# Head sums of squares: the two halves of the tokens in different columns of the array

## The chip, the cores and the metric

The kernel runs on one core of one Trainium2 chip. The metric is the device time of one execution in microseconds (us): the median of 3 runs of the kernel before is 2346.19 us (2345.56 to 2347.66). TensorE is called PE in the profile, its weight loads PEld, VectorE is DVE, ScalarE is ACT, SyncE is SP, GpSimd is POOL.

## The reference

One layer of a hybrid block on 1024 tokens of width 1024: adaLN, RMSNorm and one wide input projection that feeds dilated-window attention and a recurrent branch (RG-LRU); both are projected, gated, merged and added to x; then an expert-choice layer of 16 SwiGLU experts. All of it is float32. What bears on this change is the norm of each query and key head and the rotation:

```python
def rms_norm(t, w):
    y = t32 * lax.rsqrt(jnp.mean(t32 * t32, axis=-1, keepdims=True) + NORM_EPS)
    return (y * w.astype(jnp.float32)).astype(t.dtype)
...
q = apply_rope(rms_norm(q.reshape(b, s, N_ATTN_HEADS, HEAD_DIM), q_norm_w), positions)
k = apply_rope(rms_norm(k.reshape(b, s, N_ATTN_HEADS, HEAD_DIM), k_norm_w), positions)
```

There are 12 query heads and 12 key heads of 64 channels. The mean of squares over a head's 64 channels is what the changed lines compute.

## The kernel before

The stages follow each other: norm, q/k/v projection (`stage_qkv`), attention, LRU, merge, output and router, experts. Each large product is done with three float32r matmuls, high by high, high by low and low by high, from weights that ACT copies to the rounded high part (`split_high`) and DVE subtracts to the low part (`split_low`). Each engine has its own instruction stream, written out in the order in which it runs; semaphores join them.

In `stage_qkv` the q and k projections come as 12 chunks j = 0 to 11 of 128 channels, so two heads a chunk. The result of a chunk has its 128 channels on the partitions and the 1024 tokens along the free axis, in two PSUM banks of 512 tokens (h = 0 and 1). For each j:

- PE, iteration j: `project(j+1)` (L298, 48 matmuls of 128x512), then `head_sums(j)` (L711), then `ada_sum(8+j)` (L351, 2 matmuls with one moving column for the adaLN vector). `head_sums(j)` multiplies the squares, kept as float32 in SBUF, by a selector of 32 columns cut from the constants, whose columns 2j and 2j+1 hold 1/64 for the chunk's two heads. Over the 12 chunks it accumulates 24 rows of means in PSUM, for h = 0 in one bank and for h = 1 in the next, both on partitions 0 to 31. Each of its two float32 matmuls stands in the trace as two weight loads and two matmul records, called passes here.
- ACT, for chunk j: waits for `project(j)` and for `head_sums(j-1)`, since there is one buffer of squares; then squares (L588), scaled copy to SBUF (L589), `split_high` of a later chunk (L276), and issues 4 DMAs (L601) that swap the rotary halves between partitions.
- DVE, iteration j: `rotate(j-1)` (L655, L656, L658; it waits for the swap's DMAs), `ada_unit(8+j)` (L338, L340), `split_low` of chunk j+2 (L285). The last `split_low` of this loop prepares the first weights of v.
- SP fetches weights of 1 MB into a ring of 3 slots (L237), each as soon as the reader of a slot has freed it.

After the loop ACT takes the square root of all means at once (L604, from both banks, 32x1024, into `rstd`), DVE the reciprocal (L670) and the split in high and low (L612 on ACT, L672 on DVE). PE meanwhile projects v for the first head group (L743, 9 token tiles of 24 matmuls), and from the seventh tile on spreads the reciprocals over the channels (`spread_one`, L731), which DVE multiplies into q and k (`normalise`, L681). In attention the scores (L844) are products of 64 rows, head s of a pair on rows 64s to 64s+63 of the array.

`proj_out(j)` is the pair of PSUM banks of a chunk, `halves` the two slices of 512 tokens, `ROWS` is 32.

Of the kernel before, what the change touches and what calls it, by code (L numbers as in the profile page):

```python
# [21 lines left out]
ACT = mybir.ActivationFunctionType  # L22
# [9 lines left out]
ROWS = 32  # L32
# [26 lines left out]
C_EPS = C_ONE + 1  # L59
# [70 lines left out]
class Build:  # L130
# [114 lines left out]
    def item(self, kind, n, i):  # L245

        raw = self.unit(kind, n)
        if kind == "xy":
            s = self.order[(kind, n)] % RAW
            return self.raw[:, s, i * D:(i + 1) * D].rearrange("p (c n) -> p c n", c=KC)  # L250
        if kind == "v":
            return raw[:, 4 * i:4 * i + 4, :]
        if kind in ("lru", "vv"):
            return raw[:, 2 * i:2 * i + 2, :]
        if kind == "out":
            return raw[:, i, :]
        return raw[:, :, i * P:(i + 1) * P]
# [254 lines left out]
def stage_qkv(b, g):  # L512
# [3 lines left out]
    nc, d = b.nc, b.dram  # L516
# [8 lines left out]
    with ExitStack() as ctx:  # L525
# [3 lines left out]
        std_ready, inverted, rstd_hi, rstd_lo = b.sem("qk_std"), b.sem("qk_rstd"), b.sem("rstd_hi"), b.sem("rstd_lo")  # L529
# [3 lines left out]
        rstd = rot[0:ROWS, :]  # L533
# [6 lines left out]
        cos, sin, square, turns, raw_qk = (spare[:, 0, :], spare[:, 1, :], spare[:, 2, :], spare[:, 3, :],  # L540
                                           spare[:, 4:6, :])
# [3 lines left out]
        ps_s = b.ps("ps_headsums", [P, 2, HALF], ctx)  # L545
        ps_r = b.ps("ps_spread", [P, HALF], ctx)
        ps_mod = b.ps("ps_mod1", [P, HALF], ctx)
        const, par_a, mod, cact, acc = g.const, g.par_a, g.mod, g.cact, g.acc
# [10 lines left out]
        halves = [slice(0, HALF), slice(HALF, T)]  # L559
        block = ctx.enter_context(nc.Block())  # L560

        @block.sync
        def _(sp):
            sp.dma_start(pos[:, :], d["positions"].to_broadcast([P, T])).then_inc(pos_in, 16)
            b.fetch_until(sp, "vv", 1)
            b.fetch_until(sp, "ada", 23)

        @block.scalar
        def _(act):
            for at in (0, ROWS):  # L570
                nc.scalar.activation(head_rows[at:at + ROWS, :, :],
                                     const[at:at + ROWS, C_ID + at:C_ID + at + n_heads].unsqueeze(2).to_broadcast(
                                         [ROWS, n_heads, HD]), ACT.Copy).then_inc(rstd_hi, 1)
            act.wait_ge(folded, 1)

            nc.scalar.activation(sin[:, :], angle[:, :], ACT.Sin, scale=const[:, C_SIGN:C_SIGN + 1]).then_inc(trig, 1)
            nc.scalar.activation(cos[:, :], angle[:, :], ACT.Abs).then_inc(trig, 1)
            act.wait_ge(trig, 2)
            nc.scalar.activation(cos[:, :], cos[:, :], ACT.Sin, scale=-1.0,
                                 bias=const[:, C_PI2:C_PI2 + 1]).then_inc(trig, 1)  # L580
            for j in range(n_qk):
                act.wait_ge(b.pair_done, item(j) + 1)
                if j >= 1:
                    act.wait_ge(sum_done, j)
                if j >= 2:
                    act.wait_ge(rotated, j - 1)
                w = (A_QN if j < QK_CHUNKS else A_KN) + j % QK_CHUNKS
                nc.scalar.activation(square[:, :], proj_out(j), ACT.Square).then_inc(sq_ready, 1)  # L588
                nc.scalar.activation(raw_qk[:, j % 2, :], proj_out(j), ACT.Identity,  # L589
                                     scale=par_a[:, w:w + 1]).then_inc(sq_ready, 1)  # L590
                if j + 2 < n_qk:
                    b.split_high(act, "qk", (j + 2) // 2, j % 2)
                else:
                    b.split_high(act, "v", 0, j % 2)

                act.wait_ge(sq_ready, 2 * j + 2)
                if j:
                    act.wait_ge(rot_read, j)
                for n in range(4):
                    dst, src = slice(32 * n, 32 * n + 32), slice(32 * (n ^ 1), 32 * (n ^ 1) + 32)  # L600
                    act.dma_start(swapped[dst, :], raw_qk[src, j % 2, :]).then_inc(swap_in, 16)  # L601
            act.wait_ge(rotated, n_qk)
            act.wait_ge(sum_done, n_qk)
            nc.scalar.activation(rstd[:, :], ps_s[0:ROWS, :, :].rearrange("p a n -> p (a n)"), ACT.Sqrt,  # L604
                                 bias=const[0:ROWS, C_EPS:C_EPS + 1]).then_inc(std_ready, 1)
            act.wait_ge(rotated, n_qk)
            for t in range(V0_TILES):
                act.wait_ge(v_ps, t + 1)
                nc.scalar.activation(g.v0[:, t, :], ps_a[:, t % 4, 0:UNIT], ACT.Copy).then_inc(v_read, 1)
                if t == lag - 4:  # L610
                    act.wait_ge(inverted, 1)
                    nc.scalar.activation(r_split[0:ROWS, :], rstd[:, :], ACT.Copy).then_inc(rstd_hi, 1)  # L612
            for i in range(2):
                b.split_high(act, "vv", 0, i)
            for i in range(2):
                b.split_high(act, "vv", 1, i)
            for t in range(4):
                act.wait_ge(v_ps, V0_TILES + t + 1)
                nc.scalar.activation(g.v12[:, t, :], ps_a[:, t, :], ACT.Copy).then_inc(v_read, 1)
            for i in range(2):  # L620
                b.split_high(act, "vv", 2, i)
            for t in range(4):
                act.wait_ge(v_ps, V0_TILES + 4 + t + 1)
                nc.scalar.activation(g.v12[:, 4 + t, :], ps_a[:, t, :], ACT.Copy).then_inc(v_read, 1)

        @block.vector
        def _(dve):
# [21 lines left out]
            def rotate(j):  # L649

                raw = raw_qk[:, j % 2, :]
                if j:
                    dve.wait_ge(rotated, j)
                dve.wait_ge(swap_in, 64 * (j + 1))
                nc.vector.tensor_tensor(rot[:, :], swapped[:, :], sin[:, :], ALU.mult).then_inc(rot_read, 1)  # L655
                chain(nc.vector.tensor_tensor(raw, raw, cos[:, :], ALU.mult))  # L656
                dve.wait_ge(rot_read, j + 1)
                nc.vector.tensor_tensor(stored(j), natural(j, rot[:, :]), natural(j, raw), ALU.add).then_inc(rotated, 1)  # L658
# [7 lines left out]
                else:  # L666
                    b.split_low(dve, "v", 0, j % 2)
            rotate(n_qk - 1)
            dve.wait_ge(std_ready, 1)
            nc.vector.reciprocal(rstd[:, :], rstd[:, :]).then_inc(inverted, 1)  # L670
            dve.wait_ge(rstd_hi, 3)
            nc.vector.tensor_tensor(r_split[ROWS:2 * ROWS, :], rstd[:, :], r_split[0:ROWS, :].bitcast(F32), ALU.subtract).then_inc(rstd_lo, 1)  # L672
# [32 lines left out]
        def _(pe):  # L705
            def head_sums(j):

                pe.wait_ge(sq_ready, 2 * j + 1)
                at = C_SEL + ROWS - 2 - 2 * j
                for h in range(2):  # L710
                    last = nc.tensor.matmul(ps_s[0:ROWS, h, :], const[:, at:at + ROWS], square[:, halves[h]],  # L711
                                            start=(j == 0), stop=(j == n_qk - 1))
                last.then_inc(sum_done, 1)

            b.project(proj_out(0), "qk", 0, 0, g.h_hi, g.h_lo)
            for j in range(n_qk):
                if j + 1 < n_qk:
                    if j:
                        pe.wait_ge(sq_ready, 2 * j)
                    b.project(proj_out(j + 1), "qk", (j + 1) // 2, (j + 1) % 2, g.h_hi, g.h_lo)  # L720
                head_sums(j)
                ada_sum(b, pe, 8 + j, acc, g.acc_free, ps_mod, const[:, C_ONE:C_ONE + 1])
# [12 lines left out]
            for t in range(V0_TILES):  # L735
                if t >= 4:
                    pe.wait_ge(v_read, t - 3)
                for c in range(KC):
# [3 lines left out]
                    for m, (a, r) in enumerate(((g.h_hi, b.hi), (g.h_lo, b.hi), (g.h_hi, b.lo))):  # L742
                        last = nc.tensor.matmul(ps_a[:, t % 4, 0:UNIT], tok(a), w(r),  # L743
                                                start=(c == 0 and m == 0), stop=(c == KC - 1 and m == 2))
# [7 lines left out]
            for k, (r, m, t) in enumerate(vv_steps):  # L752
# [6 lines left out]
                for c in range(2):  # L759
                    chunk = vv_chunk(m) + c  # L760

                    def tok(h):
                        by_class = h[:, chunk, :].rearrange("p (a u c) -> p c u a", u=2, c=4)
                        return by_class[:, tile // 2, tile % 2, :]
                    w = lambda ring: b.shaped(ring, "vv", vv_item(m) % 2)[:, c, :]
                    for x, (a, y) in enumerate(((g.h_hi, b.hi), (g.h_lo, b.hi), (g.h_hi, b.lo))):
                        last = nc.tensor.matmul(ps_a[:, t, :], tok(a), w(y), start=(first and c == 0 and x == 0),
                                                stop=(final and c == 1 and x == 2))
# [1317 lines left out]
```

## Time and profile before

| | |
|---|---|
| median of 3 runs | 2346.19 us |
| the profiled execution | 2344.26 us |
| its span, first to last instruction | 2342.4 us |
| mean granted clock of TensorE in it | 0.963 |
| PE busy | 2125.1 us, 91% of the span |
| DVE busy | 1625.8 us, 69% |
| ACT busy | 1272.5 us, 54% |

The durations come from the one profiled execution, so sums are made against its 2342.4 us, with 1.9 us around it. Of a matmul the start is what counts: its end is modelled, and the next starts before it. The granted clock is 1.00 at 2.4 GHz and 0.50 at 1.2 GHz.

### The profile page before, as it was taken

What the parts mean: (1) busy time and instruction counts of PE and PEld (TensorE: products, weight loads), DVE (VectorE), ACT (ScalarE), POOL (GpSimd) and SP (SyncE); (2) the same over time, 40 slices, a digit from 0 to 9 for tenths busy, and PEclk for the clock granted to TensorE, in tenths of its full rate; (3) what the DMA queues carried; (4) which work ended last, traced back from release to release, by engine and by line L of the source; (5) the groups of instructions that cost most, each with busy time, mean ns of one, the idle gap of its engine ahead of it and who ended that gap; (6) DMA issues with size and microseconds to landing.
All of it is one profiled execution on the core that took longest, in us unless ns stands there. A gap on an engine that the chain in (4) does not pass through costs nothing. (4 is left out here: it accounts for less than half of the span.)

```text
span 2342.4 us, 25454 instructions
## 1 busy us (share of the span) xinstructions
PE 2125.1 (91%) x9747; PEld 1727.5 (74%) x9747; DVE 1625.8 (69%) x1577; ACT 1272.5 (54%) x1153; POOL 118.0 (5%) x89
## 2 busy tenths in 40 slices
PE   3999989799989999899279999999999999999997
PEld 2676778688867777677267778877787877788776
DVE  7666536558885323243668888888888888888886
ACT  5322136257874311222247777777777777677764
POOL 0000000000000000000300000000000000000000
PEclk9999989899999999999679999999999999999999
DMA  7455120011103111222479999999999999999993
GB/s 283 126 153 169 47 72 2 21 41 41 59 3 108 59 41 56 71 89 92 170 299 348 367 380 383 360 357 359 384 377 370 360 357 367 378 379 365 360 356 117
DMA packets 245847, 510.83 MB, mean 218 GB/s; under 512 B 7660, under 2 KB 65304, under 8 KB 245784
## 3 DMA queue, kind: packets, MB, share of 16 engines
q1 hardware_dynamic: 237552, 485.75, 55.5%
q0 software_dynamic: 5632, 17.83, 2.9%
q10 hardware_dynamic: 2600, 6.38, 1.1%
q8 instruction: 43, 0.70, 0.1%
q14 instruction: 20, 0.16, 0.0%
HBM read 486.87 MB, written 16.78 MB: 215 GB/s over the span
## 5 line engine op out<-in xcount | busy, mean ns | idle before, releaser
L1895 DVE TENSOR_TENSOR h_lo<-tiles,h_hi 128x2048 fp32r<-128x2048 f32 x252 | 566.2, 2288 | 113.3 <-ACT h_hi L1864 113.2
L1864 ACT ACTIVATE h_hi<-tiles 128x2048 fp32r<-128x2048 f32 x252 | 469.1, 1910 | 195.4 <-PE ps_down L1969 102.9
L1969 PE MATMUL ps_gu<-h_hi,moe_x_hi 128*128 128x512 f32 x1024 | 405.0, 395 | 2.5 <-DVE moe_x_lo L1901 2.5
L1969 PE MATMUL ps_gu<-h_lo,moe_x_hi 128*128 128x512 f32 x1024 | 400.1, 391 | 0.0
L1969 PE MATMUL ps_gu<-h_hi,moe_x_lo 128*128 128x512 f32 x1024 | 400.0, 391 | 0.0
L1895 DVE TENSOR_TENSOR h_lo<-late_tiles,h_hi 128x2048 fp32r<-128x2048 f32 x128 | 287.6, 2289 | 55.0 <-ACT h_hi L1864 55.0
L1864 ACT ACTIVATE h_hi<-late_tiles 128x2048 fp32r<-128x2048 f32 x128 | 238.3, 1910 | 115.1 <-PE ps_gu L1969 65.9
L1969 PEld LDWEIGHTS ps_gu<-h_hi,moe_x_hi 128*128 128x128 f32 x1024 | 193.0, 188 | 41.8 <-issue 2.9
L1969 PEld LDWEIGHTS ps_gu<-h_hi,moe_x_lo 128*128 128x128 f32 x1024 | 193.0, 188 | 41.5
L1969 PE MATMUL ps_down<-h_hi,moe_h_hi 128*128 128x512 f32 x512 | 204.2, 399 | 19.6 <-DVE moe_h_lo L1901 19.6
L1969 PEld LDWEIGHTS ps_gu<-h_lo,moe_x_hi 128*128 128x128 f32 x1024 | 193.1, 189 | 38.8
L298 PE MATMUL ps_projected<-h_hi,hi_ring 128*128 128x512 f32 x512 | 201.7, 394 | 6.9 <-ACT tiles L1411 4.5
L298 PE MATMUL ps_projected<-h_lo,hi_ring 128*128 128x512 f32 x512 | 200.7, 392 | 0.0
L298 PE MATMUL ps_projected<-h_hi,lo_ring 128*128 128x512 f32 x512 | 200.7, 392 | 0.0
L1969 PE MATMUL ps_down<-h_lo,moe_h_hi 128*128 128x512 f32 x512 | 199.6, 390 | 0.0
L1969 PE MATMUL ps_down<-h_hi,moe_h_lo 128*128 128x512 f32 x512 | 199.5, 390 | 0.0
L285 DVE TENSOR_TENSOR lo_ring<-tiles,hi_ring 128x1024 fp32r<-128x1024 f32 x68 | 82.9, 1223 | 162.8 <-ACT hi_ring L276 162.7
L1969 PEld LDWEIGHTS ps_down<-h_hi,moe_h_hi 128*128 128x128 f32 x512 | 96.1, 188 | 44.9 <-DVE h_lo L1895 24.6
L276 ACT ACTIVATE hi_ring<-tiles 128x1024 fp32r<-128x1024 f32 x68 | 71.2, 1052 | 98.4 <-PE ps_projected L298 48.6
L298 PEld LDWEIGHTS ps_projected<-h_hi,hi_ring 128*128 128x128 f32 x512 | 97.1, 190 | 30.2 <-issue 5.1
L298 PEld LDWEIGHTS ps_projected<-h_lo,hi_ring 128*128 128x128 f32 x512 | 97.2, 190 | 20.3
L298 PEld LDWEIGHTS ps_projected<-h_hi,lo_ring 128*128 128x128 f32 x512 | 97.0, 190 | 20.4
(292 smaller groups left out, 3288.4 us busy)
## 6 DMA issues: line engine op xcount, KB each, us to landing
tiles<-in_w_gate SPq DMA_DIRECT2D x48, 2048.0 KB, 8.7
tiles<-in_w_up SPq DMA_DIRECT2D x48, 2048.0 KB, 9.1
tiles<-in_w_down SPq DMA_DIRECT2D x32, 2048.0 KB, 10.5
late_tiles<-in_w_down SPq DMA_DIRECT2D x32, 2048.0 KB, 10.1
late_tiles<-in_w_gate SPq DMA_DIRECT2D x16, 2048.0 KB, 8.2
late_tiles<-in_w_up SPq DMA_DIRECT2D x16, 2048.0 KB, 7.7
tiles<-in_w_ada SPq DMA_DIRECT2D x24, 1024.0 KB, 7.1
tiles<-in_w_in SPq DMA_DIRECT2D x17, 1024.0 KB, 5.3
```

Of the source, the lines that this page charges most:

```text
L276: self.nc.scalar.activation(self.shaped(self.hi, kind, k % 2), self.item(kind, n, i), ACT.Copy).then_inc(self.hi_ready, 1)
L285: self.nc.vector.tensor_tensor(self.shaped(self.lo, kind, k % 2), self.item(kind, n, i), self.shaped(self.hi, kind, k % 2).bitcast(F32), A ...
L298: last = self.nc.tensor.matmul(out2[:, cols], w[:, c, :], a[:, c, cols], start=(c == 0 and w is whi and a is moving_hi), stop=(c == KC - 1 ...
L1864: nc.scalar.activation(half(w_hi[:, t % 2, :], i), half(raw_tile(g, t), i), ACT.Copy).then_inc(hi_ready, 1)
L1895: nc.vector.tensor_tensor(half(w_lo[:, t % 2, :], i), half(raw_tile(g, t), i), half(w_hi[:, t % 2, :], i).bitcast(F32), ALU.subtract).then ...
L1969: ins = nc.tensor.matmul(bank, a, w[:, t % 2, cols], start=start and m == 0, stop=stop and m == 2)
```

## The change

For h = 1 the sums go to partitions 32 to 63 of their bank instead of 0 to 31, and so to another 32 columns of the array. The selector, the squares and the order of the matmuls stay. The square root is taken by two instructions, one for each half of the tokens, each from its own partitions and both into partitions 0 to 31 of `rstd`; the reciprocal waits for both.

```diff
-            nc.scalar.activation(rstd[:, :], ps_s[0:ROWS, :, :].rearrange("p a n -> p (a n)"), ACT.Sqrt,
-                                 bias=const[0:ROWS, C_EPS:C_EPS + 1]).then_inc(std_ready, 1)
+            for h in range(2):
+                nc.scalar.activation(rstd[:, halves[h]], ps_s[ROWS * h:ROWS * (h + 1), h, :], ACT.Sqrt,
+                                     bias=const[0:ROWS, C_EPS:C_EPS + 1]).then_inc(std_ready, 1)
...
-            dve.wait_ge(std_ready, 1)
+            dve.wait_ge(std_ready, 2)
...
                 for h in range(2):
-                    last = nc.tensor.matmul(ps_s[0:ROWS, h, :], const[:, at:at + ROWS], square[:, halves[h]],
+                    last = nc.tensor.matmul(ps_s[ROWS * h:ROWS * (h + 1), h, :], const[:, at:at + ROWS], square[:, halves[h]],
                                             start=(j == 0), stop=(j == n_qk - 1))
```

## Rows read from the trace of the kernel before

**Rows 1.** Busy time by stretch: stretch, then PE, PEld, DVE, ACT, POOL, clock, DMA.
```profile
75.00:225.00 150.00, 149.37 (x624) 108.25 (x624) 98.55 (x135) 37.54 (x38) 0.00 (x0) 1.00 0.51 151
...
1200.00:2342.00 1142.00, 1093.49 (x4960) 893.97 (x4958) 967.34 (x555) 820.14 (x552) 78.08 (x45) 1.00 0.95 356
```

**Rows 2.** The chain that ended last, shares of the span by engine.
```profile
PE 43%; issue 3%; ACT 1%; DVE 1%; DMA 0%; DVEq 0%; POOL 0%; ACTq 0%; POOLq 0%
```

**Rows 3.** Waits from 75 to 225 us: total us, times, longest.
```profile
ACT v L588 <- PE ps_headsums L711: 112.4, 11, 10.4
DVE rotated L655 <- DMA v<-v: 36.9, 10, 5.9
```

**Rows 4.** The head sums' line: ns min/median/max, first and last start.
```profile
L711 PE MATMUL ps_headsums<-v,const x48: 592/592/617, 87.1 to 225.5; 128*32 128x512 f32 x48
```

**Rows 5.** Timeline of one iteration's end: start, length, engine, operation.
```profile
86.83 0.39 PE L298 MATMUL ps_proj<-h_hi,lo_ring 128*128 128x512 f32 x1
87.14 0.14 PEld L711 LDWEIGHTS ps_headsums<-v,const 128*32 128x32 f32 x2 [0.35 <-issue]
...
88.98 0.61 PE L351 MATMUL ps_mod<-const,acc 128*128 128x1 f32 x4
...
89.45 0.48 PE L298 MATMUL ps_proj<-h_hi,hi_ring 128*128 128x512 f32 x1
```

**Rows 6.** Timeline of PE, the next iteration's head sums.
```profile
100.55 1.90 PE L711 MATMUL ps_headsums<-v,const 128*32 128x512 f32 x4
```

**Rows 7.** Timeline of PE, one set of attention scores.
```profile
346.98 0.37 PE L844 MATMUL ps_s<-k_rest,tiles 64*128 64x128 f32 x1
346.99 0.48 PE L844 MATMUL ps_s<-tiles 64*128 64x256 f32 x1
347.19 0.27 PE L844 MATMUL ps_s<-k_rest,tiles 64*128 64x128 f32 x1
347.30 0.81 PE L844 MATMUL ps_s<-tiles 64*128 64x256 f32 x6
...
348.06 0.27 PE L844 MATMUL ps_s<-k_rest,tiles 64*128 64x128 f32 x1
```

**Rows 8.** Timeline of all engines at the end of the loop.
```profile
209.72 1.03 ACT L588 ACTIVATE v<-ps_proj 128x1024 f32<-128x1024 f32 x1 [10.42 <-PE ps_headsums L711]
...
211.35 0.37 SPq L237 DMA_DIRECT2D tiles<-in_w_ada  x1
...
211.79 2.45 ACTq L601 DMA_DIRECT2D v<-v  x4
...
219.55 1.23 DVE L655 TENSOR_TENSOR rotated<-v 128x1024 f32<-128x1024 f32 x1 [5.59 <-DMA v<-v]
...
227.62 1.22 DVE L285 TENSOR_TENSOR lo_ring<-tiles,hi_ring 128x1024 fp32r<-128x1024 f32 x1
...
228.89 0.39 PE L743 MATMUL ps_proj<-hi_ring,h_hi 128*128 128x256 f32 x1 [0.53 <-DVE lo_ring L285]
```

**Rows 9.** Timeline of another swap and the weight fetch behind it.
```profile
158.19 2.56 ACTq L601 DMA_DIRECT2D v<-v  x4
158.95 0.37 SPq L237 DMA_DIRECT2D tiles<-in_w_ada  x1
...
166.23 1.22 DVE L655 TENSOR_TENSOR rotated<-v 128x1024 f32<-128x1024 f32 x1 [5.87 <-DMA v<-v]
```

**Rows 10.** Timeline after the loop: square root, low part, first spread.
```profile
233.94 1.11 ACT L604 ACTIVATE rotated<-ps_headsums,const 32x1024 f32<-32x1024 f32 x1 [4.95 <-DVE k_rest L658]
...
242.75 1.22 DVE L672 TENSOR_TENSOR rstd_split<-rotated,rstd_split 32x1024 fp32r<-32x1024 f32 x1 [1.12 <-ACT rstd_split L612]
...
249.24 0.49 PE L731 MATMUL ps_spread<-rstd_split,head_rows 64*128 64x512 f32 x1
```

**Rows 11.** A stall of PE in the v projection, and the stretch from 259 us.
```profile
261.58 1.02 PE L351 MATMUL ps_mod<-const,acc 128*128 128x1 f32 x4 [4.69 <-DVE acc L340]
...
259.00:266.00 7.00, 4.30 (x11) 3.04 (x11) 4.65 (x7) 0.00 (x0) 0.00 (x0) 0.52 0.46 148
```

## The prediction

> **What bounds the kernel now.** I read the stretches first, then the chain of waits, then the waits inside the stretch that the change touches, then the timeline. The stretches show PE busy for 149.37 of 150 us while the q and k chunks run, at full clock, and for 1093 of 1142 us in the experts; the chain that ended last gives PE 43% of the span and no other engine more than 1% [rows 1, 2]. The reader is to see that PE sets the pace at both places, so that time taken out of the first moves all that follows, if nothing else becomes late between them. In the waits of the loop two stand out: ACT waits 11 times for the head sums, 112.4 us in all, and DVE 10 times for the swap's DMAs, 36.9 us [rows 3]. Neither is the pace: both engines wait for PE or for what PE released. PE itself has no wait in the list above 0.7 us.
>
> **What the head sums cost.** All 48 passes have one form, 128 rows by 32 columns, 592 ns in the median with a modelled end [rows 4]. Their price is read from starts. The first weight load of a set starts at 87.14 and the next product, the adaLN sum, at 88.98: 1.84 us for four passes, of which each takes (88.98 - 87.14 - 0.1) / 4 = 0.43 us, and about 0.1 us is the change of form at the end. At the front the last 128x512 matmul started at 86.83, and as such matmuls follow each other every 0.227 us (48 of them in the 10.9 us from 89.45 to about 100.3), the load comes some 0.09 us after it was done [rows 5, 6]. So the change from 128 columns to 32 and back is already paid, about 0.1 us each time, and the edit adds no such step: both halves keep the form 128 by 32. The period of the loop is 100.55 - 87.15 = 13.40 us [rows 5, 6].
>
> **What the new place of the second half does.** Today the four passes, first half high and low, second half high and low, use the same 32 columns and stand one behind the other. With the second half in the next 32 columns, two passes can run beside each other. No row of this kernel has two matmuls in different columns. The nearest is the attention's scores, six float32 products in 64-row pieces, alternately in the lower and the upper half of the rows. There the first pass of the second product starts at 346.99, about 10 ns after the first pass of the first (346.98) and 0.2 us before that one's second pass (347.19). The set has eight passes of 256 columns and four of 128; at the head sums' 0.43 us for 512 columns these are 8 x 0.215 + 4 x 0.107 = 2.15 us one behind the other, and they take 348.06 + 0.107 - 346.98 = 1.19 us [rows 7]. Pieces in different rows therefore run in full beside each other, each piece with its own order.
>
> Bounds for one set of head sums: as in the scores, two steps of 0.43 us instead of four, a gain of 0.86 us; in the other direction no overlap, and a weight load that can't be hidden at the change of columns, at the price of the form change above, a loss of 0.1 to 0.2 us. I take 0.86 us, since the scores are the nearest row: same type, same two passes, same kind of small product.
>
> The Trainium skill would make less of it. "TensorE: Matmul & The Clock Gate", section "Part 3: Packing small matmuls — row/col tiling", says that matmuls start and end strictly in program order, whichever piece of the array they use. By that rule the second half could start only with the first half's second pass, three steps instead of four, and the gain of a set would be 0.43 us. The start at 346.99 ahead of 347.19 disagrees with it for rows; no run here shows columns. The same section gives 2.38 times for three products side by side in columns, which speaks for an overlap as such.
>
> **How many of the 12 sets count.** In the loop each set lies between two projections on PE, which does not wait. At the end it is otherwise. PE starts v at 228.89 after `split_low` on DVE [rows 8], and this is the last piece of one unbroken chain: head sums of chunk 9 end, ACT squares chunk 10 (209.72), the swap is issued (211.79), it lands and DVE rotates (219.55), then adaLN and `split_low` (227.62) back to back. Sets 0 to 9 stand ahead of this chain, so ten count. Sets 10 and 11 run on PE while this chain runs, and PE waits for it: they count nothing. 10 x 0.86 = 8.6 us.
>
> The swap in this chain takes 219.55 - 211.79 = 7.76 us from issue to use. A weight fetch was issued 0.44 us ahead of it [rows 8]. That fetch hangs on the rotation one period earlier, and the swap on PE; with a period shorter by 0.86 us the swap is issued 0.4 us ahead of the fetch. That case exists too: a swap 0.76 us ahead of a fetch took 166.23 - 158.19 = 8.04 us [rows 9]. So this step loses about 0.2 us, and does not gain. Sum: 8.6 - 0.2 = 8.4 us.
>
> Inside the loop nothing else becomes late. DVE is busy 98.55 of 150 us and ACT 37.54 [rows 1]; with a period of 12.54 us instead of 13.40 DVE would be at 70% instead of 66%. `split_low` for a chunk is done 19 us (228.84 - 209.72) after the head sums that start its chain [rows 8], and PE needs it two periods after them, 25.1 us then.
>
> **The square root** becomes two of 32x512 instead of one of 32x1024, 1.11 us [rows 10]. Two fixed parts instead of one cost between nothing and, if each took as long as the whole, 1.1 us; I take 0.2 us. It is hidden: the low part that ends this chain starts at 242.75 and takes 1.22 us, and PE uses it first at 249.24, so 5.3 us are free [rows 10]. The v tiles that ACT has to clear behind it have as much: seven tiles of 24 matmuls lie between 228.89 and 249.24, 0.121 us a matmul, so PE reuses the first bank after four tiles at 240.5, when the square root has been done for 5 us. Since v starts as early as the DVE chain allows and the square root hangs on the rotation just behind it, this cover moves with the rest. If it were gone, the cost would be these 0.2 us, at most 1.1. The second half read from partitions 32 to 63 and written to 0 to 31 has no row; it would have to cost over 5 us to be seen.
>
> **The clock** gives the scatter. After v PE waits 4.69 us for adaLN, and the clock from 259 to 266 us is 0.52: (1 - 0.52) x 7 / 0.5 = 6.7 us at 1.2 GHz, of which PE works at most 4.3 [rows 11]. All work that comes after the loop shifts by 8 us, and a lower level may begin earlier or later against its stall: each one met or missed by PE's work is worth at most half of 6.7, 3.4 us. I count it as zero on average, with 3 us either way.
>
> Forecast: the profiled span 2342.4 becomes about 2334.0. The median of the runs lies 1.93 us above the profiled execution's 2344.26; with the same distance, 2346.19 - 8.4 = 2337.8 us.
>
> **Rivals.** (1) Program order binds: three steps a set, 0.43 us x 10 = 4.3 us, 2341.9. For it: one stream of instructions, and the two halves share all 128 rows, which the scores' pieces do not. Against it: the scores. This is what the rule of the Trainium skill quoted above gives. (2) Nothing runs side by side: passes through the same rows stay in line, 2346.2. For it: the same sharing of rows, on which no row speaks. (3) It gets slower: at the step from the first to the second 32 columns, 12 times, PE drains and loads anew, as it does at the change of form. Price 0.1 to 0.2 us in each of the ten sets that count, 1 to 2 us, about 2348. If two streams through the same rows also held each other up so that a pass took twice 0.43 us, it would be 1.7 us a set, 17 us, 2363. It decides from the point at which a pair takes longer than its two passes one behind the other. For it speaks only that no row excludes it; against it that the first two weight loads of a set start within 0.14 us, so loads do run ahead of matmuls [rows 5]. (4) The overlap comes and is worth more: if the swap of chunk 10 landed sooner once it stands ahead of the fetch, v could start earlier until PE's own work is the limit: adaLN 0.5, projection 10.9, a set 1.8, the squares 1.0, a set 1.9 and adaLN 0.6 after 209.6 give 226.3, so at most 2.6 us less than 228.89, and 2335. The late landing in [rows 9] speaks against it; I hold it inside the forecast's range.
>
> **Numbers.** Full overlap 0.50 (with (4)), program order 0.22, nothing 0.18, slower 0.10. The likeliest one's own range is 2333.5 to 2341.5. The 8 in 10 range has to take in rival (1) and most of (2): 2333 to 2347. A measurement of this kernel can tell 0.2%, 4.7 us, from no change. Faster by more: 0.43 from the full overlap, 0.10 from program order with a lucky clock, 0.01 from the rest, 0.54. Slower by more: 0.05, nearly all from the stronger form of (3). The same: 0.41.
>
> **What the profile after would show.** Right: two passes of a set start within some ns, the first weight load to the adaLN sum takes 0.98 us, the period is 12.54 us, v starts near 220.5, and the square root's two pieces end over 4 us before the first spread. Program order: 1.41 us and 12.97 us. Nothing: 1.84 us or more. The forecast is wrong if sets are shorter and v does not start earlier by ten times that, or if the gain at v is lost by later stalls or lower clock.

## The result and the profile after

The changed kernel takes 2336.05 us (median of 8 runs, 2334.19 to 2337.58), the kernel before beside it 2345.88 us (8 runs, 2341.48 to 2358.26). The ratio is 0.9949, 95% interval 0.9928 to 0.9971: 0.5% faster, clear of no change. It is taken over all the runs and is not the quotient of the two medians, which is 0.9958; the same holds for the ratios below. The forecast was 2337.8 us.

The profiled execution has a span of 2335.5 us, 6.9 us less than the 2342.4 of before, at a mean clock of 0.961. Its head sums, in the timeline (start, length, engine, line, operation, shapes, count):

```profile
87.13 0.14 PEld L713 LDWEIGHTS ps_headsums<-v,const 128*32 128x32 f32 x4 [0.35 <-issue]
87.13 1.05 PE L713 MATMUL ps_headsums<-v,const 128*32 128x512 f32 x4
...
88.11 0.61 PE L351 MATMUL ps_mod<-const,acc 128*128 128x1 f32 x4
...
88.29 1.03 ACT L588 ACTIVATE v<-ps_proj 128x1024 f32<-128x1024 f32 x1 [6.57 <-PE ps_headsums L713]
```

All four weight loads now fall within 0.14 us, where two did before [rows 5], and from the first of them to the adaLN sum it is 88.11 - 87.13 = 0.98 us instead of 1.84. The first two passes of the next set alone, from a narrower window:

```profile
99.64 0.62 PE L713 MATMUL ps_headsums<-v,const 128*32 128x512 f32 x2
```

Two passes together take 0.62 us, the modelled length that a single one had at most [rows 4]: they run side by side. The period is 99.64 - 87.13 = 12.51 us instead of 13.40 [rows 6]. The line's own summary shows the same 48 passes, 592 to 617 ns each with a median of 605, none longer than before.

At the end of the loop, where [rows 8] stood, the timeline of all engines reads:

```profile
200.95 1.03 ACT L588 ACTIVATE v<-ps_proj 128x1024 f32<-128x1024 f32 x1 [9.54 <-PE ps_headsums L713]
...
203.01 2.48 ACTq L601 DMA_DIRECT2D v<-v  x4
...
210.57 1.23 DVE L656 TENSOR_TENSOR rotated<-v 128x1024 f32<-128x1024 f32 x1 [5.39 <-DMA v<-v]
...
214.54 1.05 PE L713 MATMUL ps_headsums<-v,const 128*32 128x512 f32 x4 [0.64 <-ACT v L588]
218.79 1.01 PE L351 MATMUL ps_mod<-const,acc 128*128 128x1 f32 x4 [3.20 <-DVE acc L340]
219.93 0.58 PE L745 MATMUL ps_proj<-hi_ring,h_hi 128*128 128x256 f32 x1
220.31 0.41 PE L745 MATMUL ps_proj<-hi_ring,h_lo 128*128 128x256 f32 x1
220.52 0.41 PE L745 MATMUL ps_proj<-lo_ring,h_hi 128*128 128x256 f32 x1
```

v starts at 219.93 instead of 228.89, 8.96 us earlier. But PE has waited 3.20 us for the adaLN unit of DVE, where in the kernel before it waited 1.66 us:

```profile
227.76 0.61 PE L351 MATMUL ps_mod<-const,acc 128*128 128x1 f32 x4 [1.66 <-DVE acc L340]
```

In the changed kernel the v matmuls then follow each other every 0.21 us instead of every 0.12: they begin at the lower clock (granted 0.50 from 218 to 219 us) and keep it until about 224.6 us. The first spread, and the square roots ahead of it, against [rows 10]:

```profile
224.23 1.39 ACT L605 ACTIVATE rotated<-ps_headsums,const 32x512 f32<-32x512 f32 x2 [4.90 <-DVE k_rest L659]
...
233.32 1.22 DVE L673 TENSOR_TENSOR rstd_split<-rotated,rstd_split 32x1024 fp32r<-32x1024 f32 x1 [1.12 <-ACT rstd_split L613]
...
242.37 0.49 PE L733 MATMUL ps_spread<-rstd_split,head_rows 64*128 64x512 f32 x1
```

The spread comes 6.87 us earlier, not 8.96: 2.1 us are given back within the v projection. From there on nothing changes. The stretches (PE, PEld, DVE, ACT, POOL, clock, DMA) are the end of the loop, attention, LRU and merge, output and router, experts:

```profile
212.00:230.00 18.00, 14.04 (x84) 11.81 (x83) 16.23 (x15) 6.38 (x8) 0.00 (x0) 0.81 0.46 147
...
327.00:443.00 116.00, 92.76 (x712) 81.64 (x712) 70.47 (x296) 60.11 (x170) 0.00 (x0) 0.88 0.00 1
443.00:985.00 542.00, 514.20 (x2177) 412.44 (x2177) 285.21 (x260) 247.26 (x252) 19.49 (x33) 0.98 0.17 53
985.00:1184.00 199.00, 136.59 (x656) 114.88 (x656) 94.41 (x154) 47.54 (x59) 20.18 (x7) 0.78 0.31 113
1184.00:2335.00 1151.00, 1102.15 (x4984) 900.93 (x4984) 967.75 (x556) 820.57 (x553) 78.07 (x45) 0.99 0.95 356
```

The clock of 0.81 in the first is an average over both levels, the lower one from the end of the 3.20 us on. The same stretches of the kernel before, each 7 us later, have PE busy for the same time within 0.2 us (92.76, 514.36, 136.41 and 1102.20 us) at the same clocks.

### The profile page after: what moved, and what is told of

It is laid out like the page before. It is cut to its first block and busy times, and to the rows that moved or that the text cites. A ratio compares the mean times of both kernels' runs of the same rounds, so it can differ in the third digit from the quotient of the medians.

```text
span 2335.5 us, 25455 instructions
## 1 busy us (share of the span) xinstructions
PE 2117.1 (91%) x9747; PEld 1727.6 (74%) x9747; DVE 1625.4 (70%) x1577; ACT 1273.0 (55%) x1154; POOL 117.9 (5%) x89
```

## Experiments

In the profiles below "attention" is the time from the first score matmul to the first projection of the next stage: 115.66 us before (from 334.51) and 115.67 us after (from 327.65). The experiments ran on several chips, and the changed kernel itself was repeated on only one of them, with the experiments on the square root and on other columns. Against the others its 2336 us comes from another chip, so differences of 1 or 2 us in a median show nothing there. In the profiles the first set starts between 85.9 and 87.7 us, so times late in the loop are best taken from that start.

**Only the two square roots.** Both halves back in columns 0 to 31, two square roots kept.

```diff
-                nc.scalar.activation(rstd[:, halves[h]], ps_s[ROWS * h:ROWS * (h + 1), h, :], ACT.Sqrt,
+                nc.scalar.activation(rstd[:, halves[h]], ps_s[0:ROWS, h, :], ACT.Sqrt,
...
-                    last = nc.tensor.matmul(ps_s[ROWS * h:ROWS * (h + 1), h, :], const[:, at:at + ROWS], square[:, halves[h]],
+                    last = nc.tensor.matmul(ps_s[0:ROWS, h, :], const[:, at:at + ROWS], square[:, halves[h]],
```

> Both halves of the head sums in columns 0 to 31 as in the kernel before; of the change only the two square roots are left. Theory A (the gain is all from the place in the array, the square root is hidden): a set takes 1.84 us again, the period is 13.40 us, v starts at 228.9, the two square roots take about 1.4 us instead of 1.1, and the time is that of the kernel before. Rival (part of the gain comes from the square root's halves): the time stays up to 2 us below the kernel before.

The timeline of PE:

```profile
86.09 1.90 PE L713 MATMUL ps_headsums<-v,const 128*32 128x512 f32 x4
87.93 0.61 PE L351 MATMUL ps_mod<-const,acc 128*128 128x1 f32 x4
...
227.71 0.39 PE L745 MATMUL ps_proj<-hi_ring,h_hi 128*128 128x256 f32 x1 [0.53 <-DVE lo_ring L285]
...
248.06 0.49 PE L733 MATMUL ps_spread<-rstd_split,head_rows 64*128 64x512 f32 x1
```

The set is 1.84 us again. 2347.59 us against 2343.31 for the kernel before on that chip, ratio 1.0005 (0.9983 to 1.0027): no gain is left, which is theory A. The interval can't exclude an effect of the square root of 2 us; the profile does. From the first set to v and to the first spread it takes 141.6 and 162.0 us, as in the kernel before (141.8 and 162.1), and in the changed kernel 132.8 and 155.2.

**Other columns.** The second half in columns 64 to 95 (`2 * ROWS * h` in place of `ROWS * h` for the first partition, in both places).

> The second half in columns 64 to 95 instead of 32 to 63. Theory A (any other group of 32 columns does): set 0.98 us, period 12.51, the time of the changed kernel. Rival (the neighbouring group is special, because two groups of 32 are served as one of 64): the set falls back towards 1.4 or 1.84 us, 4 to 9 us slower than the changed kernel.

```profile
85.94 1.05 PE L713 MATMUL ps_headsums<-v,const 128*32 128x512 f32 x4
86.92 0.61 PE L351 MATMUL ps_mod<-const,acc 128*128 128x1 f32 x4
```

A set of 0.98 us and 2336.07 us, beside 2336.27 us for the changed kernel itself on that chip (below): the neighbouring group is not special. Nor is it the PSUM bank that parts the halves: in the kernel before they went to two banks already, in the same columns, and the set took 1.84 us.

**What runs ahead of what.** A third matmul in each set, issued between the two, in the first half's columns.

```diff
                 for h in range(2):
+                    if h:
+                        nc.tensor.matmul(ps_r[0:ROWS, :], const[:, at:at + ROWS], square[:, halves[0]], start=True, stop=True)
                     last = nc.tensor.matmul(ps_s[ROWS * h:ROWS * (h + 1), h, :], const[:, at:at + ROWS], square[:, halves[h]],
```

> The changed kernel with a third matmul in each set: first half in columns 0 to 31, the first half again in columns 0 to 31 (another bank, result not used), then the second half in columns 32 to 63. Theory A (each column group runs on its own, past work that waits for the other group): two steps of the second half beside four of the first columns, a set of 1.84 us, and the second half's first pass starts with the set. Theory B (passes start in program order, and may only overlap): the second half can't start before the fourth pass does, five steps, 2.27 us.

Timeline of PE and ACT; L714 is the added matmul, L715 the first and the last of the three:

```profile
86.56 0.63 PE L715 MATMUL ps_headsums<-v,const 128*32 128x512 f32 x2
...
86.56 1.06 PE L715 MATMUL ps_headsums<-v,const 128*32 128x512 f32 x4
87.44 1.02 PE L714 MATMUL ps_spread<-v,const 128*32 128x512 f32 x2
...
88.39 0.61 PE L351 MATMUL ps_mod<-const,acc 128*128 128x1 f32 x4
88.58 1.03 ACT L588 ACTIVATE v<-ps_proj 128x1024 f32<-128x1024 f32 x1 [6.80 <-PE ps_headsums L715]
```

Theory A. The last matmul of the program starts with the first, at 86.56, and both of its passes have started by 87.03 (the four end at 87.62, of which the last pass is 0.59); the one issued ahead of it starts only at 87.44, when its columns are free. The set takes 1.83 us. Starts are thus not in program order across column groups. The signal still comes in order: it hangs on the last matmul, whose own stream is over near 87.46, and ACT goes on at 88.58, 0.28 us after the added one's second pass is through (87.87 + 0.43 = 88.30). In the changed kernel ACT goes on 0.27 us after its last pass (87.59 + 0.43 = 88.02, 88.29). So one signal on the last matmul of a set still stands for all of them. The one execution took 2343.6 us, which fits sets as long as before.

**Four column groups.**

```diff
-                for h in range(2):
-                    last = nc.tensor.matmul(ps_s[ROWS * h:ROWS * (h + 1), h, :], const[:, at:at + ROWS], square[:, halves[h]],
+                for q in range(4):
+                    last = nc.tensor.matmul(ps_s[ROWS * q:ROWS * (q + 1), q // 2, q % 2 * UNIT:(q % 2 + 1) * UNIT],
+                                            const[:, at:at + ROWS], square[:, q * UNIT:(q + 1) * UNIT],
```

> The head sums of each chunk as four matmuls of 256 tokens, in the columns 0 to 31, 32 to 63, 64 to 95 and 96 to 127 of the array, and four square roots. Theory A (each group of 32 columns runs its own sequence, the shared 128 rows hold nobody up): all four run side by side, two steps of 0.21 us, a set takes about 0.55 us from its first weight load to the adaLN sum instead of 0.98, the loop's period falls from 12.51 to about 12.1 us, v starts about 4.3 us earlier than with two columns, near 215.6 us, and the time is about 4 us below the changed kernel. Theory B (the shared rows carry two streams and no more): two pairs one behind the other, a set stays at about 0.98 us and the time does not move.

```profile
86.68 0.64 PE L714 MATMUL ps_headsums<-v,const 128*32 128x256 f32 x8
87.25 0.61 PE L351 MATMUL ps_mod<-const,acc 128*128 128x1 f32 x4
...
98.78 0.64 PE L714 MATMUL ps_headsums<-v,const 128*32 128x256 f32 x8
...
214.28 1.01 PE L351 MATMUL ps_mod<-const,acc 128*128 128x1 f32 x4 [4.03 <-DVE acc L340]
215.42 0.58 PE L747 MATMUL ps_proj<-hi_ring,h_hi 128*128 128x256 f32 x1
```

Eight passes in a set of 0.57 us, a period of 12.10 us, v at 215.42: theory A, and four streams through the same 128 rows hold nobody up. From the first set to v it takes 128.74 us instead of 132.80, which is 4.1 us, ten times 0.41. 2332.5 us (6 runs), 0.9931 of before (0.9906 to 0.9955), 3.6 us below the first measurement of the changed kernel. The wait of PE ahead of v has grown to 4.03 us, and v again begins at the lower clock: its first matmul stands with 0.58 us, and the first spread comes 22.4 us after it (237.83), as in the changed kernel.

**The wait filled.** The changed kernel, with useless matmuls in the 3.20 us.

```diff
                 head_sums(j)
+                if j == n_qk - 1:
+                    for _ in range(14):
+                        nc.tensor.matmul(ps_r[:, :], g.h_hi[:, 0, 0:P], g.h_hi[:, 0, 0:HALF], start=True, stop=True)
                 ada_sum(b, pe, 8 + j, acc, g.acc_free, ps_mod, const[:, C_ONE:C_ONE + 1])
```

> The changed kernel with 14 more matmuls of 128x512 behind the last head sums, 14 x 0.227 = 3.2 us of useless work in the place where PE waits 3.20 us for adaLN; their result is not used. Theory A (that wait is what the lower clock from 217.9 to 224.7 us follows): the clock stays at 1.00 there, v starts at about 219.9 as before, the first spread comes at about 240.3 instead of 242.4, and the time is about 2 us lower, though PE does more. Theory B (the lower clock has nothing to do with this wait): the lower clock stays, the first spread stays at 242.4, no change.

Timeline of PE, then the stretches of the end of the loop and of attention:

```profile
215.61 3.51 PE L726 MATMUL ps_spread<-h_hi 128*128 128x512 f32 x14
218.98 0.61 PE L351 MATMUL ps_mod<-const,acc 128*128 128x1 f32 x4
220.12 0.39 PE L748 MATMUL ps_proj<-hi_ring,h_hi 128*128 128x256 f32 x1 [0.53 <-DVE lo_ring L285]
220.34 0.28 PE L748 MATMUL ps_proj<-hi_ring,h_lo 128*128 128x256 f32 x1
220.46 0.28 PE L748 MATMUL ps_proj<-lo_ring,h_hi 128*128 128x256 f32 x1
...
240.47 0.49 PE L736 MATMUL ps_spread<-rstd_split,head_rows 64*128 64x512 f32 x1
```

```profile
212.00:230.00 18.00, 16.84 (x115) 13.81 (x114) 16.23 (x15) 6.73 (x9) 0.00 (x0) 1.00 0.46 147
325.00:450.00 125.00, 101.65 (x713) 89.52 (x714) 70.58 (x296) 60.12 (x171) 0.26 (x1) 0.82 0.00 1
```

At its place theory A holds: the clock stays at 1.00, the v matmuls come every 0.12 us, and the first spread at 240.47 instead of 242.37. The time does not follow: the median is 2339.61 us (12 runs, 2337.05 to 2347.84), more than the changed kernel's instead of 2 us less. Attention took 124 us in this profile instead of 116, at a clock of 0.82 instead of 0.88, with the same work and PE busy for 101.65 us instead of 92.76. I had not looked there.

**v first.** The low part of the first v weights ahead of the loop's last adaLN unit.

```diff
-                ada_unit(b, dve, chain, 8 + j, acc, g.acc_free, cact)
+                if j < n_qk - 1:
+                    ada_unit(b, dve, chain, 8 + j, acc, g.acc_free, cact)
...
                     b.split_low(dve, "v", 0, j % 2)
+                if j == n_qk - 1:
+                    ada_unit(b, dve, chain, 8 + j, acc, g.acc_free, cact)
...
-                ada_sum(b, pe, 8 + j, acc, g.acc_free, ps_mod, const[:, C_ONE:C_ONE + 1])
+                if j < n_qk - 1:
+                    ada_sum(b, pe, 8 + j, acc, g.acc_free, ps_mod, const[:, C_ONE:C_ONE + 1])
...
+                if t == 1:
+                    ada_sum(b, pe, 7 + n_qk, acc, g.acc_free, ps_mod, const[:, C_ONE:C_ONE + 1])
```

> The changed kernel, with DVE's low part of the first v weights ahead of the last adaLN unit of the loop, and PE's adaLN sum for it behind the second v tile instead of ahead of v. Theory A (v waits for the DVE chain): the low part starts when its high part is there, 216.4 us, v starts at about 217.7 instead of 219.9, and the wait of PE shrinks from 3.2 us in one piece to about 2.1 us. Gain 2.2 us, and 2 us more if the clock then stays up: 2.2 to 4.3 us below the changed kernel. Rival: the square root, pushed back by about 1.5 us, becomes late for the fifth v tile or the first spread, and the gain is lost.

```profile
217.31 0.58 PE L749 MATMUL ps_proj<-hi_ring,h_hi 128*128 128x256 f32 x1 [2.15 <-DVE lo_ring L285]
...
239.33 0.49 PE L737 MATMUL ps_spread<-rstd_split,head_rows 64*128 64x512 f32 x1
```

```profile
324.00:452.00 128.00, 105.59 (x712) 93.33 (x712) 70.67 (x296) 59.81 (x169) 0.00 (x0) 0.79 0.00 1
```

The same again. v at 217.31 and the first spread at 239.33 are 2.6 and 3.0 us earlier than in the changed kernel, of which 0.4 us are an earlier start of the loop, and the square root is in time. The clock did not stay up, though PE waits only 2.15 us: the v matmuls come every 0.21 us until 220.04. The median is 2342.24 us (11 runs): four of them lie from 2334.8 to 2335.3, about 1 us below the changed kernel where 2.2 to 4.3 were expected, seven from 2341.1 to 2345.9. The profile is one of the long ones, with attention at 128 us and a clock of 0.79.

**Both together.** Four column groups and v first.

> Four column groups and the earlier low part together. If the two gains are independent: 4.3 us and 2.2 to 4.3 us, so 6.5 to 8.6 us below the changed kernel, a median near 2329. Rival: the wait of PE ahead of v grows with shorter sets (those of chunks 10 and 11 do not count), the clock falls there, and only the 4.3 us and 2.2 us remain, less 2 us.

```profile
212.98 0.39 PE L751 MATMUL ps_proj<-hi_ring,h_hi 128*128 128x256 f32 x1 [2.57 <-DVE lo_ring L285]
```

v at 212.98, attention 115.5 us in the profile, and 2329.74 us (6 runs, 2327.66 to 2331.02), 0.9918 of before (0.9894 to 0.9941), the fastest of all. That is 6.3 us below the 2336.05 of the changed kernel, a little less than the 6.5 to 8.6 of the first theory and more than the 4.5 of the rival. In the profile the two gains at the first spread, 4.5 and 3.0 us, add up to nearly the 7.1 found here (235.27 against 242.37), with the lower clock for 3 us of v in this version too. No run of these six is a long one, while with v first alone seven of eleven are. What makes attention long is what the delays ask.

**Delays ahead of attention.** The changed kernel with 3 or 6 matmuls at the end of the q/k/v stage.

```diff
+            pe.wait_ge(normalised, n_spread)
+            for _ in range(3):
+                nc.tensor.matmul(ps_r[:, :], g.h_hi[:, 0, 0:P], g.h_hi[:, 0, 0:HALF], start=True, stop=True)
```

> The changed kernel with 3 more matmuls of 128x512 at the end of the q/k/v stage on PE (result not used), about 1.3 us of delay ahead of attention at the lower clock that rules there. Theory A (the time of attention depends on the moment at which it is reached, since its stalls of PE then meet the clock differently): attention, 115.7 us from the first score to the first projection of the next stage, becomes 120 to 128 us in the profile, as in the runs with the filled stall and with v first, and the runs spread up to 10 us upwards. Theory B (those runs were long for another reason): attention stays at 115 to 116 us and the time rises by the 1.3 us alone.

> The same with 6 more matmuls, about 2.6 us of delay. Theory A: another moment again, attention anywhere between 115 and 128 us; if it is back at 115 to 116 us the cost is not monotone in the delay, which theory B can't give. Theory B: 2.6 us above the changed kernel, attention at 115 to 116 us.

The way into attention with 6, on PE (L769 is the last product of the q/k/v stage, L784 the added ones, L849 the first score):

```profile
325.68 0.63 PE L769 MATMUL ps_proj<-lo_ring,h_hi 128*128 128x512 f32 x1
326.46 1.66 PE L784 MATMUL ps_spread<-h_hi 128*128 128x512 f32 x6
328.41 0.34 PE L849 MATMUL ps_s<-k_rest,tiles 64*128 64x128 f32 x1 [0.30 <-PEq L525]
```

The delays are smaller than planned. From the last product to the first score it takes 2.73 us here, 2.12 with 3 (327.22 to 329.34) and 1.57 in the changed kernel (326.08 to 327.65), where PE waits for part of that time anyway. The six need 1.66 us, so they ran mostly at the higher clock. They delay attention by 1.2 us and the three by 0.55 us, not by 2.6 and 1.3.

Attention in the profiles with 3 and with 6, and of the latter 28 us alone:

```profile
329.00:445.00 116.00, 92.82 (x714) 81.86 (x714) 70.39 (x296) 59.91 (x170) 0.23 (x1) 0.89 0.00 1
```

```profile
328.00:456.00 128.00, 105.52 (x713) 93.15 (x712) 70.66 (x296) 59.80 (x169) 0.00 (x0) 0.79 0.00 1
...
336.00:364.00 28.00, 27.27 (x125) 23.86 (x124) 10.49 (x51) 10.08 (x30) 0.00 (x0) 0.50 0.00 1
```

With 3 the profile has attention at 115.5 us, and eight of ten runs lie from 2336.6 to 2338.9; the two others are at 2346.2 and 2350.2. With 6, five runs lie from 2340.8 to 2343.6, one at 2345.0 and four from 2349.6 to 2351.7, and attention took 127.8 us in the profile. There PE works through 28 us of it at the lower clock (0.50), with 125 matmuls; the same piece of the changed kernel, 335 to 363 us, has 219 matmuls at 0.96, and the profile of v first shows the long form too (126 matmuls at 0.50 from 332 to 360 us).

The medians of 3 and 6, on one chip, differ by 6.3 us for 0.6 us more delay, which theory B can't give. For 3 the expectation of theory A for the profile did not come true; two of its ten runs are as long as it would make them. So what precedes attention changes its length, by up to 12 us between profiles, and one kernel shows both lengths from run to run. But theory A is not shown as it stands: the added matmuls shift the moment and also give PE work just ahead of attention, and these runs don't separate the two. The rule stays open.

**The changed kernel again, and the square root three times.** The latter adds about 2.8 us to ACT's chain.

```diff
+            for again in range(3):
+                if again:
+                    act.wait_ge(std_ready, 2 * again)
```

> The changed kernel itself beside the others on one chip: 9 to 12 us below the kernel before, with the lower clock behind the 3.2 us wait as in the first profile.

> The changed kernel with the two square roots done three times over, about 2.9 us more on ACT behind the last rotation. Theory A (about 5 us are free there): the low part of the reciprocals starts near 236.2 instead of 233.3, the first spread stays at 242.4, no change of the time. Rival (the chain through the square root ends last): about 3 us slower.

The changed kernel takes 2336.27 us (9 runs, 2334.68 to 2338.8), ratio 0.9958 (0.9943 to 0.9974), 7.0 us below the 2343.31 of before: less than the 9 to 12 expected, the 2336 of the first measurement itself repeated. With three times the square root, the timelines of PE, ACT and DVE are:

```profile
219.30 0.58 PE L748 MATMUL ps_proj<-hi_ring,h_hi 128*128 128x256 f32 x1
...
223.59 4.22 ACT L608 ACTIVATE rotated<-ps_headsums,const 32x512 f32<-32x512 f32 x6 [5.42 <-DVE k_rest L662]
...
235.52 1.22 DVE L676 TENSOR_TENSOR rstd_split<-rotated,rstd_split 32x1024 fp32r<-32x1024 f32 x1 [1.12 <-ACT rstd_split L616]
...
241.06 0.49 PE L736 MATMUL ps_spread<-rstd_split,head_rows 64*128 64x512 f32 x1
```

The pieces take 4.22 us instead of 1.39, and the first spread still comes 21.8 us after the start of v (22.4 in the changed kernel). 2337.19 us (7 runs), ratio 0.9948, 0.9 us above the changed kernel on the same chip, which is within the scatter of either and not the 3 us of the rival: theory A, the square root is hidden. Its profile is its slowest run, with attention at 120.0 us.

## Why the prediction was right, point by point

- *What bounds.* Right: PE sets the pace in the loop, and the 6.87 us that are there at the first spread reach the end unchanged (6.9 us of span).
- *The price of a set.* Right: 0.98 us forecast, 0.98 measured. The reading of the scores was the deciding step: pieces in different rows run beside each other, each with its own order, and pieces in different columns do so too. The rival by program order (1.41 us a set) falls with the profile and with the third matmul; by the Trainium skill's rule, "TensorE: Matmul & The Clock Gate", section "Part 3: Packing small matmuls — row/col tiling", starts and ends are both in program order. The trace agrees for the signal of the end (88.58) and not for the starts, 86.56 for the last issued against 87.44 for the one issued before it.
- *Nothing side by side, and slower.* Both rivals fall: no drain shows between the column groups, and even eight passes in four groups cost no more than two steps.
- *Ten sets count.* Right: the last set that counts starts at 207.73 in the kernel before and at 199.80 in the one after. Nine periods give 9 x 0.88 = 7.9, the tenth set 0.86.
- *The swap of chunk 10.* I forecast that it would lose 0.2 us; from issue to rotation it took 210.57 - 203.01 = 7.56 us instead of 7.76 and gained 0.2. The swap (203.01) stands 0.05 us ahead of the weight fetch (203.06), not 0.4. 7.9 + 0.86 + 0.2 = 8.96, the whole of v's earlier start, where 8.4 was forecast.
- *The square root.* 1.39 us for both pieces, 0.28 more where I took 0.2, and hidden.
- *The clock.* This is the step that failed, the term "zero on average, with 3 us either way". It was wrong twice. First, the forecast said itself that sets 10 and 11 shorten while the chain that they wait for does not; it did not say that PE then waits in one piece longer, 3.20 us instead of 1.66, and that the lower clock can follow. It does, and takes back 2.1 us (22.4 us from v to the first spread instead of 20.35), as the filled wait shows, where these 20.35 us return. This is inside the 3 us, but it is a one-sided loss of this edit and not scatter. Second, the term took its price from one stall, with 6.7 us at 1.2 GHz. In the long attentions the lower clock lasts 28 us in one piece, and their length moves by up to 12 us.

The result of 2336.05 lies 1.75 us below the forecast by two differences that work against each other, and that it comes so near is luck. The mechanism gives 6.9 us where I had 8.4; from 2346.19 that alone would make 2339.3, still inside the range. The medians differ by 9.8 us because the runs of the kernel before spread over a lower group and a long upper tail. Of the 8 beside the result five lie from 2341.5 to 2346.2, median 2343.3, which is 7.3 us above the changed kernel's 2336.05. Of the 27 beside its repetition 19 lie from 2341.3 to 2346.7, median 2342.7, 6.4 us above its 2336.27 on that chip. Both are near the 6.9 of the profiles.

What fits the upper runs is attention at the lower clock: the kernel with only the square roots has PE's order of before, its profile shows attention at 120.1 us, and its span is 2347.4. No profile of the kernel before itself caught such a run. That the changed kernel's 17 runs, 2334.2 to 2338.8, hold none is measured. Whether this is owed to the moment at which it reaches attention stays open, and so some 3 us of the 9.8 are not explained by the mechanism of the edit.

## What to carry to other kernels

Small products like these, which use at most 32 columns of the array, can be put in different groups of 32 by the partitions of their output, and then run side by side even when they share all rows; four groups made a set of head sums 0.57 us instead of 1.84. What is won ahead of a wait for another engine can make PE's wait longer, and the lower clock behind it can take a part back (2.1 of 9.0 us here), so look for waited-for work that can be moved forward with it, as in the fastest version; there the lower clock came all the same. Where stages stall PE often, a change of a few us upstream has to be judged by several runs and by the length of each stage, since one stage alone moved by 12 us here.

## What was unexpected of the hardware

- Matmuls in another column group start ahead of matmuls issued before them (86.56 against 87.44), yet the signal on the last issued comes only after all have ended (ACT at 88.58, the added one's stream over at 88.30).
- Four float32 streams through the same 128 rows run at full speed: eight passes of 256 columns in 0.57 us.
- The same attention work took between 114.7 and 128.0 us in the profiles, at mean clocks from 0.89 to 0.79 where read, in kernels that differ only ahead of it. Six more matmuls, which delay it by 1.2 us, went with 127.8 us in one profile.
